# Recurrent block: gate product on VectorE in one operation, first convolution step on ScalarE, order of a unit's parts from a table

## What is computed

```
xb, gate = split(h @ w_in)                    # (2048, 1024) each
xb = causal_depthwise_conv(xb, conv_w, conv_b)   # width 4
r = sigmoid(block_diag_linear(xb, w_a, b_a))
i = sigmoid(block_diag_linear(xb, w_x, b_x))     # 16 blocks of 64
log_a = -8 * r * softplus(-lam);  a = exp(log_a)
u = sqrt(1 - exp(2 * log_a)) * (i * xb)
hseq[t] = a[t] * hseq[t-1] + u[t]             # over 2048 positions
y = (hseq * gelu(gate)) @ w_out
```

## Time and profile before

| | us |
|---|---|
| median of 3 runs | 2742.05 (2738.2 to 2743.55) |
| the profiled execution, its own time | 2738.65 |
| span of its slowest core | 2737.1 |
| spans of the 8 cores | 2720.6 to 2737.1 |
| busy PE / DVE / ACT / POOL | 2567.1 / 1179.1 / 789.9 / 347.9 |
| activation table loads | 51, 65.4 us |
| first wait of the recurrent stage to its first tile's products | 1971.32 to about 2224 |

### The profile page before, as it was taken

How to read it: one execution, slowest core, us unless ns; L and a number is a source line. 1 busy time by engine, 2 the same in 40 slices (tenths; PEclk the granted TensorE clock), 3 DMA queues, 4 the chain that set the end, 5 groups by cost and what they waited for, 6 DMA issues and landing times.

```text
span 2737.1 us, 30678 instructions; the slowest of 8 cores (2720.6 to 2737.1 us)
## 1 busy us (share of the span) xinstructions
PE 2567.1 (94%) x12224; PEld 1114.7 (41%) x12224; DVE 1179.1 (43%) x1851; ACT 789.9 (29%) x1141; POOL 347.9 (13%) x340
## 2 busy tenths in 40 slices
PE   6999999788888799999999999999978889999999
PEld 2444444333333234444444444444423334444444
DVE  4234234455555453423425243243567853424423
ACT  5110113255556542011014101102356632010010
POOL 0100000111111101000000100000048630000000
PEclk9999999899999899999999999999989999999999
DMA  6521310111001103231221412211111113222223
GB/s 151 85 38 25 54 28 15 27 32 16 16 16 21 30 1 61 37 54 28 34 35 16 74 27 43 45 29 28 20 21 20 18 27 61 40 50 32 34 35 119
DMA packets 56095, 105.85 MB, mean 39 GB/s; under 512 B 4624, under 2 KB 5776, under 8 KB 55952
## 3 DMA queue, kind: packets, MB, share of 16 engines
q0 software_dynamic: 44288, 83.90, 18.6%
q1 hardware_dynamic: 11664, 19.99, 2.5%
HBM read 179.37 MB, written 8.39 MB: 69 GB/s over the span
## 4 chain that ended last, share of the span: by engine, by line
PE 85%; DVE 6%; ACT 5%; POOL 2%; DMA 1%; issue 1%; SPq 0%; ACTq 0%; POOLq 0%; DVEq 0%
PE ps L294 85%; ACT arena L303 4%; DVE arena L306 3%; POOL arena L310 2%; DVE arena L310 1%; DMA arena<-xT 1%; DVE arena L317 1%; DVE arena L672 0%; SPq L332 0%; DVE arena L314 0%; DMA arena<-attn_wout 0%; ACT L303 0%; POOL arena L317 0%; DVE arena L850 0%; DMA arena<-lru_wout 0%
## 5 line engine op out<-in xcount | busy, mean ns | idle before, releaser
L294 PE MATMUL ps<-arena 128*128 128x512 bf16 (+6 forms) x12224 | 2567.1, 376 | 166.5 <-ACT arena L303 50.2
L294 PEld LDWEIGHTS ps<-arena 128*128 128x128 bf16 (+2 forms) x12224 | 1114.7, 100 | 1618.4 <-issue 222.3
L303 ACT ACTIVATE arena<-ps 128x512 bf16<-128x512 f32 (+5 forms) x680 | 444.9, 661 | 1698.3 <-PE ps L294 1653.7
L310 DVE TENSOR_TENSOR arena<-arena,ps 128x512 bf16<-128x512 bf16 x352 | 241.9, 688 | 951.6 <-PE ps L294 950.8
L306 DVE SCALAR_TENSOR_TENSOR arena<-ps,arena 128x512 f32<-128x512 f32 (+1 forms) x560 | 415.3, 742 | 222.6 <-PE ps L294 220.5
L303 ACT ACTIVATE arena<-arena 128x512 bf16<-128x512 f32 (+4 forms) x322 | 229.0, 742 | 160.2 <-PE ps L294 58.1
L310 POOL TENSOR_TENSOR arena<-arena 128x512 bf16<-128x512 f32 (+2 forms) x112 | 195.3, 1754 | 368.0 <-PE ps L294 258.5
L448 POOL DMA_DIRECT2D arena<-ffn_win x88 | 62.5, 710 | 1253.6 <-PE ps L294 1226.9
L306 DVE SCALAR_TENSOR_TENSOR arena<-arena,ps 128x512 bf16<-128x512 f32 x192 | 133.9, 742 | 33.7 <-ACT ps L303 33.7
L310 DVE TENSOR_TENSOR arena<-arena 128x512 bf16<-128x512 bf16 (+3 forms) x188 | 86.6, 473 | 91.9 <-ACT arena L303 90.0
L454 POOL DMA_DIRECT2D arena<-ffn_wout x88 | 48.5, 557 | 396.7 <-PE ps L294 396.1
(11 more groups left out here) (20 smaller groups left out, 87.6 us busy)
## 6 DMA issues: line engine op xcount, KB each, us to landing
arena<-ffn_win POOLq DMA_DIRECT2D x88, 512.0 KB, 5.3
arena<-ffn_wout POOLq DMA_DIRECT2D x88, 256.0 KB, 6.0
arena<-xT SPq DMA_DIRECT2D x32, 256.0 KB, 13.1
outT<-arena SPq DMA_DIRECT2D x32, 256.0 KB, 2.9
arena<-attn_win POOLq DMA_DIRECT2D x8, 768.0 KB, 7.8
...
```

The lines of the kernel that those rows point to most:

```text
L294: self.P.op("pe", lambda e: e.matmul(out_ap, lhsT, rhs, start=start, stop=stop), reads=reads, writes=[self.ps_t[bank]])
L303: self.P.op("act", lambda e: e.activation(out=out, in_=in_, func=func, **kw), reads=reads, writes=writes)
L310: self.P.op(eng, lambda e: e.tensor_tensor(out=out, in0=in0, in1=in1, op=op), reads=reads, writes=writes)
```

## The change

Three things. `MUL1` becomes one SCALAR_TENSOR_TENSOR on DVE instead of two operations on POOL. The first operation of `CONV` becomes its own part, `CONV0`, an ACTIVATE with function Identity, scale and bias columns, on ACT. And the written loop over the chunks is replaced by a table, `LRU_X`, that gives each part a moment for the even and for the odd unit, counted in pairs; all (part, unit) are sorted by `k // 2` plus that moment and issued in that order. XB and GM are now two parts each (a, b), as is BD. The loads of weights are issued when given parts have been issued.

```
+LRU_X = {
+    "XBa": (-0.6142, -0.0846), "XBb": (-0.3745, -0.0298), "CONV0": (-0.3128, -0.0098), "CONV": (-0.1804, 0.2877),
...
+        def CONV0(k):
+            c, m = units[k]
+            xc, xct = buf("xc", k)
+            self.act(xc, xb2, AF.Identity, XBk + [self.cv_t], [xct], scale=self.cvcol(CV_CW + 24 + c), bias=self.cvcol(CV_CB + c))
+
         def CONV(k):
...
-            self.ts(xc, xb2, cw[3], cb, ALU.mult, ALU.add, XBk + [self.cv_t], [xct])
...
-            self.ts(thx, thx, 1.0, 1.0, ALU.add, ALU.mult, [thxt], [thxt], eng="pool")
-            self.tt(thx, thx, xc, ALU.mult, [thxt, xct], [thxt], eng="pool")
+            self.stt(thx, thx, 1.0, xc, ALU.add, ALU.mult, [thxt, xct], [thxt])
...
-        CONV(0)
-        GM(1, (1,))
-        BD(0)
-        XB(1)
...
+        pulled = {("XBa", 0), ("XBb", 0), ("GMa", 0), ("GMb", 0), ("GMa", 1)}
+        events = sorted((k // 2 + LRU_X[nm][k % 2], i, nm, k) for k in range(nu) for i, nm in enumerate(stage)
+                        if (nm, k) not in pulled)
+        load_out((0,), 0)
+        done_ = set()
+        lds = [((1, 2), 1, [("GMb", 11), ("XBb", 11)]), ((3, 4), 2, [("GMb", 13), ("XBb", 13)]),
+               ((5, 6), 3, [("SCAN", 12)]), ((7,), 4, [("SCAN", 13)])]
+        nload = 3
+        for _, _, nm, k in events:
+            stage[nm](k)
+            done_.add((nm, k))
+            if nload < NCH and ("GMb", 2 * nload - 5) in done_ and ("XBb", 2 * nload - 5) in done_:
+                load_w(nload)
+                nload += 1
+            if lds and all(x in done_ for x in lds[0][2]):
+                load_out(*lds.pop(0)[:2])
```

More of the change, by code:

```diff
@@ L25 @@
 ENGS = ("pe", "act", "dve", "pool", "sp")
+LRU_X = {
+    "XBa": (-0.6142, -0.0846), "XBb": (-0.3745, -0.0298), "CONV0": (-0.3128, -0.0098), "CONV": (-0.1804, 0.2877),
+    "BDa": (0.0662, 0.6127), "BDb": (0.2393, 0.7086), "GMa": (0.1262, 0.8437), "GMb": (0.3505, 0.9146),
+    "GELU": (0.9596, 0.9453), "EXP2": (0.4190, 0.8519), "MIN": (0.6622, 1.0394), "EXP1": (0.6443, 1.4153),
+    "SQ": (0.8759, 1.1710), "MUL1": (0.3486, 0.9067), "MUL2": (0.8944, 1.3471), "SCAN": (1.1234, 1.4503),
+    "Y": (1.1674, 1.7036),
+}
 class T:
@@ L1139, in oadd @@
                     [self.ps_t[bank], self.x_t[c][t]], [self.x_t[c][t]])
[L1141 to L1189, removed]
-            if c == NCH - 1:
-                load_out((5, 6), 3)
-                load_out((7,), 4)
@@ new lines, in lru @@
+        stage = {"XBa": lambda k: XB(k, (0,)), "XBb": lambda k: XB(k, (1,)), "CONV0": CONV0, "CONV": CONV,
+                 "BDa": lambda k: BD(k, (0,)), "BDb": lambda k: BD(k, (1,)),
+                 "GMa": lambda k: GM(k, (0,)), "GMb": lambda k: GM(k, (1,)), "GELU": GELU, "EXP2": EXP2, "MIN": MIN,
+                 "EXP1": EXP1, "SQ": SQ, "MUL1": MUL1, "MUL2": MUL2, "SCAN": SCAN, "Y": Y}
+        pulled = {("XBa", 0), ("XBb", 0), ("GMa", 0), ("GMb", 0), ("GMa", 1)}
+        events = sorted((k // 2 + LRU_X[nm][k % 2], i, nm, k) for k in range(nu) for i, nm in enumerate(stage)
+                        if (nm, k) not in pulled)
@@ L1196, in lru @@
             omm(0, c, obank[c], range(0, 7))
-        SCAN(k0)
-        Y(k0)
-        SCAN(k1)
-        Y(k1)
         for c in range(8):
```

## The result

The changed kernel takes 2674.1 us, the kernel before 2742.05 us: a ratio of 0.9754, with a 95% interval from 0.9732 to 0.9776. That is 68 us less; 60 were forecast.

The account below looks back on a forecast made before the run. It took a closed loop of TensorE, POOL and DVE, with POOL's work in it, as the bound. End mark 1998.2 + 6 x 22.6 + 30.3 = 2164.1 instead of 2224.4; 2742.05 - 60.3 = 2681.8, say 2682 us; range 2673 to 2707.

Parts of the forecast that it names:

- Start: Start of the recurrent stage: TensorE idles from 1969.6, and the walk puts BDa(2) at 1998.2 us.
- the split of the gain: Of the forecast gain, about 11.6 + 2.7 us at the stage's end, the rest from six or seven periods.
- Period: Steady time per channel pair in the recurrent stage: ACT's 21.7 us plus semaphore delays, 22.6 us.
- the loop of banks 0 and 1: XB, CONV0, the steps of CONV, then XB of the next unit: 19.7 us per channel pair.
- mixed loop: From SQ of an even unit through MUL2, scan, convolution, TensorE's pieces and EXP2 to the next even SQ: 21.3 us.
- Rival (b): DVE still stands until POOL operations end: a pair takes at most 26.8 us, 2707 us in all; chance 17%.
- Table loads: On ACT, four activation-table loads per pair where before there were three, about 58 in the page instead of 51.
- (c): Each of four table loads holds ACT 1.28 us longer: 27.7 us a pair, 2712 us in all; chance 2%.
- (d): An extra table load around each tanh group, 9 a pair: 29.1 us a pair, 2721 us in all; chance 2%.
- Rings: none costs: Buffer waits of GELU and EXP2 for Y, and of xc(o+2) for MUL1(o), were claimed to cost nothing.
- End: From BDa(14) through the 64 output products: 30.3 us, with the 11.6 us weight wait and slow products gone.
- Rival (e): Slower than before: TensorE at its lower 1.2 GHz level for the whole stage, 2792 us; chance 3%.

## Why the prediction was right, step by step

- **The bound of before.** That TensorE waited for DVE and DVE for POOL's loop is supported: taking MUL1 from POOL in the table's order is worth 39 us, the earlier release of `xc` among them. But opening the loop is not enough, as MUL1 alone in the old order shows.
- **Start.** I had BDa(2) at 1998.2. It starts 3.4 us behind 1995.54, which is 1998.0 on the clock of before, since this trace reaches the stage 1 us later. The walk was right. By the marks above I had 9.4 us less for the start and measured 9.5; the sentence with the split of the gain leaves the start out.
- **Period.** Forecast 22.6, measured 21.06: six times 1.5 us is 9.2 us of the error. The term that failed is "ACT never stands, so the period is its 21.7 us plus semaphore delays". The 21.7 us counted each ACTIVATE with its whole row; instructions that follow each other overlap (two tanh take 1.26 us, not 1.38) and ACT's row is 20.85 us busy. The 0.9 us of delays was not there either. And the loop that does bind, nine pieces with CONV0 and CONV, is on no list of mine: I had the loop of banks 0 and 1 (19.7) without the pieces that TensorE runs between an XB and the next. My mixed loop of 21.3 holds three of the nine pieces, and SQ and the SCAN.
- **CONV0** took 1.20 us, above both of my bounds, 1.02 and 1.16. The bounds were a GELU from PSUM without columns and an EXP with columns from SBUF; it has both.
- **MUL1** took 1.22 us, as I chose (1.3).
- **Collisions.** MIN is still held once a pair, 2.2 us, and a halo step for 0.6; DVE is busy for 19.2 us of 21.06 and can bear it. Rival (b) was the right worry for another kernel: with MUL1 on POOL the period is 27.3 us, in part by a collision.
- **Table loads.** Four a pair, 59 in all (58 forecast), without anything beside them. Rivals (c) and (d) are out.
- **"Rings: none costs"** was right for the changed kernel only because MUL1 is on DVE. That `xc` is released early looks like the larger part of what the move of MUL1 buys: the wait for it is 4.50 of the 6.2 us a period.
- **End.** The loads of the output weights no longer hold TensorE. But the possible hold of unit 15's halo, which I had left inside the range at no cost, came true: 3.63 us, and with it the part behind BDa(14) took 34.2 instead of 30.3 us (BDa(14) at 2121.89 + 3.4; the 64th product 2.9 us before 2162.36, as it was before 2227.30). About half of the 3.9 us is that wait, which stands with 2.0 us in my walk; the other half is the low clock behind it, for which the sum had no term. The two errors, -9.2 and +3.9, leave the sum 5.6 us short: 65.9 measured between the marks, 60.3 forecast. That they have opposite signs is luck.
- **Clock.** 0.97 in the stage, and 1.00 in the steady part. Rival (e) had nothing to stand on there; behind the 3.63 us wait the clock did fall, to a mean of 0.72 for the first 10 us.

What the prediction did not see is how narrow the ground is. I argued each of the three parts as a small gain by itself. By the runs, the order alone gives 18 us (a third each at the start, in the periods and at the end), MUL1 alone costs 5, CONV0 alone costs 51, and together they give 68.
